# Two-block network on one core: attention pairs pipelined between dense units, output projections in a new order of units

## What is computed

```python
def first_block(x, c, ...):
    for i in range(DEPTH):
        mod = silu(c) @ ada_w[i] + ada_b[i]
        shift, scale, gate = jnp.split(mod, 3)
        h = rms_norm_f32(x, norm_g[i]) * (1.0 + scale) + shift
        out = retention_mixer(h, ...) if i == 0 else chunked_attention_mixer(h, ...)
        x = x + gate * out
...
def chunked_attention_mixer(h, w_in, q_g, k_g, rel_table, w_out):   # 16 heads of 128
    q, k, v, g = jnp.split(h @ w_in, 4, axis=-1)
    q, k = rms_norm_f32(q, q_g), rms_norm_f32(k, k_g)               # per head
    s = q @ k.T * scale + bias            # a chunk of 64 sees itself and 8 chunks before
    o = softmax(s) @ v * silu(g)
    return o @ w_out                      # 2048 -> 1024
...
        hm = rms_norm(x, norm_mlp[l]) @ mlp_w1[l]                   # 1024 -> 4096
        x = x + jnp.square(jax.nn.relu(hm)) @ mlp_w2[l]             # 4096 -> 1024
```

## Time and profile before

| | us |
|---|---|
| Time of the kernel, median of 3 | 2114.42 (2105.43 to 2114.66) |
| Profiled execution, its own time | 2116.99 |
| Its span from the first to the last instruction | 2114.9 |
| PE busy | 1928.5 (91%) |
| POOL busy | 1093.8 (52%) |
| DVE busy | 787.0 (37%) |
| ACT busy | 464.1 (22%) |
| Mean granted clock of TensorE | 0.941 |

### The profile page before, as it was taken

The page is one execution under the profiler, slowest core; times in us unless marked ns, Lnnn a source line. Parts: engine busy times, 40 slices in busy tenths (PEclk is TensorE's granted clock), DMA queues, the critical chain, the costliest instruction groups (busy, mean ns, idle before and its releaser), DMA issues.

```text
span 2114.9 us, 27134 instructions
## 1 busy us (share of the span) xinstructions
PE 1928.5 (91%) x9694; PEld 1580.0 (75%) x9694; DVE 787.0 (37%) x1413; ACT 464.1 (22%) x933; POOL 1093.8 (52%) x856
## 2 busy tenths in 40 slices
PE   4699999989899999999989899989899879999998
PEld 3588887868777877778768676877777658787776
DVE  4615323155423122322231384796433463102300
ACT  2211112100212122212220115644303322101200
POOL 2345454458443435343426557874063467667752
PEclk8799999999899999999999998999997989999999
DMA  8322222247222222221312331210021123233321
GB/s 285 127 70 75 69 84 65 79 139 253 70 81 68 60 69 80 67 63 55 89 49 79 85 89 50 61 29 23 1 90 50 40 80 99 82 97 90 99 81 48
DMA packets 276375, 172.92 MB, mean 82 GB/s; under 512 B 5792, under 2 KB 269856, under 8 KB 274272
## 3 DMA queue, kind: packets, MB, share of 16 engines
q1 hardware_dynamic: 269136, 148.92, 24.2%
q10 hardware_dynamic: 7184, 23.27, 3.1%
HBM read 169.93 MB, written 2.10 MB: 81 GB/s over the span
## 4 chain that ended last, share of the span: by engine, by line
PE 80%; DVE 12%; ACT 3%; issue 2%; DMA 1%; POOL 1%; DVEq 0%; ACTq 0%; POOLq 0%
PE acc L368 18%; PE acc L369 17%; PE acc L370 17%; PE st L401 3%; PE acc L390 3%; PE acc L391 3%; PE acc L392 3%; PE ob L1302 2%; PE ob L1234 2%; DVE conv_out L1974 2%; PE bc L434 2%; PE sc L1296 1%; DVE hn L482 1%; DMA x_tok<-in_x 1%; DVE att_scores L1916 1%
## 5 line engine op out<-in xcount | busy, mean ns | idle before, releaser
L664 POOL TENSOR_SCALAR wh<-raw 128x1024 fp32r<-128x1024 f32 x232 | 255.6, 1102 | 856.9 <-PE acc L370 535.5
L667 POOL TENSOR_TENSOR wl<-raw,wh 128x512 fp32r<-128x512 f32 x464 | 643.5, 1407 | 19.4
L368 PE MATMUL acc<-hh,wh 128*128 128x512 f32 x1120 | 458.3, 409 | 44.0 <-DVE ang L1813 13.9
L369 PE MATMUL acc<-hl,wh 128*128 128x512 f32 x1120 | 446.7, 399 | 0.0
L370 PE MATMUL acc<-hh,wl 128*128 128x512 f32 x1120 | 446.3, 398 | 0.0
L368 PEld LDWEIGHTS acc<-hh,wh 128*128 128x128 f32 x1120 | 216.6, 193 | 97.1 <-issue 45.3
L370 PEld LDWEIGHTS acc<-hh,wl 128*128 128x128 f32 x1120 | 216.7, 193 | 47.2
L369 PEld LDWEIGHTS acc<-hl,wh 128*128 128x128 f32 x1120 | 216.9, 194 | 43.8 <-issue 1.7
L368 PE MATMUL acc<-Yh,wh 128*128 128x512 f32 x512 | 205.2, 401 | 18.2 <-DVE mod L1794 8.2
L369 PE MATMUL acc<-Yl,wh 128*128 128x512 f32 x512 | 204.6, 400 | 0.0
L370 PE MATMUL acc<-Yh,wl 128*128 128x512 f32 x512 | 204.2, 399 | 0.0
(11 more groups left out here) (386 smaller groups left out, 2684.2 us busy)
## 6 DMA issues: line engine op xcount, KB each, us to landing
raw<-in_att_w_in SPq DMA_DIRECT2D x64, 512.0 KB, 4.0
raw<-in_mlp_w SPq DMA_DIRECT2D x64, 512.0 KB, 4.0
raw<-in_ret_w_in SPq DMA_DIRECT2D x48, 512.0 KB, 3.9
ada_w<-in_ada_w ACTq DMA_DIRECT2D x8, 1536.0 KB, 8.2
raw<-in_w_in SPq DMA_DIRECT2D x23, 512.0 KB, 3.8
ada_w<-in_ada_w SPq DMA_DIRECT2D x8, 1024.0 KB, 16.4
raw<-in_ret_w_out SPq DMA_DIRECT2D x16, 512.0 KB, 3.7
raw<-in_att_w_out SPq DMA_DIRECT2D x16, 512.0 KB, 3.6
```

Of the source, the lines that this page charges most:

```text
L368: e.matmul(bank[:, :], wh[:, s, k, :], rhs_high(k), start=(start and k == 0), stop=False)
L369: e.matmul(bank[:, :], wh[:, s, k, :], rhs_low(k), start=False, stop=False)
L664: e.tensor_scalar(wh[:, s, :, :], raw[:, s, :, :], 1.0, 1.0, ALU.mult, ALU.mult).then_inc(high_done, 1)
L667: low = e.tensor_tensor(wl[:, s, k0:k0 + KT // 2, :], raw[:, s, k0:k0 + KT // 2, :], wh[:, s, k0:k0 + KT // 2, :].bitcast(F32), ALU.subtract)
```

## The change

**Attention.** TensorE's scores, transposes and value products no longer stand in rows of their own but in gaps between the units. In a turn: unit 0, last two scores of the pair before and seven transposes of its first head; unit 1, sums, three transposes; unit 2, sums, value product of the first head, seven transposes of the second; unit 3, sums, three transposes; first quarter of `tok`, sums; second quarter, value product of the second head, spread; two quarters, spread, two scores; unit 6, two scores; unit 7, two scores of the second head. The transposes go through `ob`, the value products into `sc`. VectorE's and ScalarE's programs are cut into the same pieces and put in the matching order. The bias of the second head is loaded a turn later than before, behind that head's exponentials.

**Output projections.** In each turn the order of units is now bank 0 lower inputs, bank 1 lower inputs, bank 0 upper inputs, bank 1 upper inputs, and the loads follow. The first turn stands ahead of the loop; its lower halves wait only for the first eight tiles of `Y`, its upper halves for the last. In `att_out` the last pair's work stands behind the first and second unit, and the upper half of bank 0 waits for the last two tiles ahead of its seventh.

```diff
-        def product(e, bank, u, c, rhs_high, rhs_low, start=True, stop=True, k1=KT, inputs=None):
+        def product(e, bank, u, c, rhs_high, rhs_low, start=True, stop=True, k1=KT, inputs=None, late=None):
...
+                if late is not None and late[0] == k:
+                    e.wait_ge(*late[1])
...
-        def out_tensor(e, tag, ready):
+        def out_tensor(e, tag, free, ready, gaps=None, late=None):
             c = U[tag]
-            e.wait_ge(*ready)
-            with e.Fori(0, KT // 2) as i:
-                PE.enter(tag, i)
-                for b in range(2):
-                    e.wait_ge(*V.at(f"{tag}x{b}", i - 1))
-                    for half in range(2):
-                        product(e, acc[b], c + i * 4 + 2 * b + half, c + 2 * b + half,
+
+            def turn(i):
+                for half in range(2):
+                    for b in range(2):
+                        if half == 0:
+                            e.wait_ge(*(free[b] if isinstance(i, int) else V.at(f"{tag}x{b}", i - 1)))
+                        if b == 0 and isinstance(i, int):
+                            e.wait_ge(*ready[half])
+                        product(e, acc[b], c + i * 4 + 2 * half + b, c + 2 * half + b,
                                 lambda k: Yh[:, 8 * half + k, :], lambda k: Yl[:, 8 * half + k, :],
...
+                        if gaps is not None and half == 0 and isinstance(i, int):
+                            gaps[b]()
+
+            turn(0)
+            with e.Fori(1, KT // 2) as i:
+                turn(i)
...
-                    e.wait_ge(unit_used, c + i * 4 + 2 * b + 2)
+                    e.wait_ge(unit_used, c + i * 4 + b + 3)
...
-                        k0 = r0 + 8 * (j % 2)
-                        load(c + i * 4, c, i, rows(w, k0, k0 + 8, (i * 2 + j // 2) * P))
+                        k0 = r0 + 8 * (j // 2)
+                        load(c + i * 4, c, i, rows(w, k0, k0 + 8, (i * 2 + j % 2) * P))
...
             with e.Fori(1, AH // 2) as i:
                 AC.enter("att_scalar", i, 1)
-                att_qk(i, "a", None)
-                att_pv(i - 1, i, "a", None)
-                att_vg(i, "a")
+                att_evict(i, "a", 0)
+                att_turned(i, "a", 0, (0, 1))
+                att_exp(i, "a", 1)
+                load_bias(1, i * 2 + 1)
+                att_evict(i, "a", 1)
+                att_turned(i, "a", 0, (2, 3))
+                att_evict(i, "a", 2)
+                att_turned(i, "a", 1, (0, 1))
+                att_high(i - 1, i, "a", 0)
+                att_evict(i, "a", 3)
+                att_turned(i, "a", 1, (2, 3))
+                att_value(i, "a", 0)
+                att_high(i - 1, i, "a", 1)
+                att_value(i, "a", 1)
+                att_gate(i, "a", 0)
+                att_exp(i, "a", 0)
+                load_bias(0, i * 2 + 2)
+                att_gate(i, "a", 1)
                 AC.leave(AH // 2 - 1)
...
-            out_tensor(e, "ret_out", V.after("r_yl3", RH))
+            out_tensor(e, "ret_out", [V.after("r_g2", RH), V.after("r_g3", RH)],
+                       [V.after("r_yl3", RH // 2), V.after("r_yl3", RH)])
...
+                    if t == "a":
+                        if j == 0:
+                            att_scores(i, t, 1, 2)
+                            att_scores(i, t, 1, 3)
+                            att_turned(i, t, 0, 0)
+                            att_turned(i, t, 0, 1)
+                        if j == 1:
+                            att_turned(i, t, 0, 2)
+                            att_turned(i, t, 0, 3)
+                        if j == 2:
+                            att_values(i, t, 0)
+                            att_turned(i, t, 1, 0)
+                            att_turned(i, t, 1, 1)
+                        if j == 3:
+                            att_turned(i, t, 1, 2)
+                            att_turned(i, t, 1, 3)
...
+                tok(e, c + 4, U["att"] + 4, f"{t}v", [AC.at(f"{t}qk2", i), AC.at(f"{t}qk3", i)],
+                    between={0: last_sums, 1: values_and_spread})
+                e.wait_ge(*V.at(f"{t}k0", i))
+                spread(e, f"{t}bc1", c0=12)
+                att_scores(i, t, 0, 0)
+                att_scores(i, t, 0, 1)
+                e.wait_ge(*AC.at(f"{t}v0", i))
+                feat(e, acc[0], c + 6, U["att"] + 6)
+                att_scores(i, t, 0, 2)
+                att_scores(i, t, 0, 3)
+                e.wait_ge(*AC.at(f"{t}v1", i))
+                feat(e, acc[1], c + 7, U["att"] + 7)
+                att_scores(i, t, 1, 0)
+                att_scores(i, t, 1, 1)
...
-            out_tensor(e, "att_out", V.at("zyl1"))
...
+            out_tensor(e, "att_out", [V.at(f"ag{b}", AH // 2 - 1) for b in range(2)],
+                       [V.at("ayl1", AH // 4), V.at("ayl1", AH // 4 + 2)], [last_scores, last_values],
+                       (6, V.at("zyl1")))
...
-                out_tensor(e, f"mlp_out{half}", V.after(f"f{half}yl3", 4))
+                out_tensor(e, f"mlp_out{half}", [AC.after(f"f{half}r{b + 2}", 4) for b in range(2)],
+                           [V.after(f"f{half}yl3", 2), V.after(f"f{half}yl3", 4)])
...
+            def att_second(i, t):
+                att_key(i, t, 1)
+                e.wait_ge(bias_in[0], i * 32 + 32)
+                for n in range(NT):
+                    att_scores(i, t, 0, n)
+                att_maxima(t, 0)
+                att_gate(i, t, 0)
+                att_normalize(i, t, 0)
+                att_gate(i, t, 1)
+                e.wait_ge(bias_in[1], i * 32 + 32)
+                for n in range(2):
+                    att_scores(i, t, 1, n)
...
             with e.Fori(1, AH // 2) as i:
                 V.enter("att_vector", i, 1)
-                att_pv(i - 1, i, "a")
-                att_vg(i, "a", i)
+                att_first(i, "a")
+                att_out_value(i, "a", 0)
+                att_low(i - 1, i, "a", 0)
+                att_roots(i, "a")
+                att_out_value(i, "a", 1)
+                att_key(i, "a", 0)
+                att_low(i - 1, i, "a", 1)
+                att_second(i, "a")
                 V.leave(AH // 2 - 1)
```

More of the change, by code:

```diff
@@ L376, in feat, with tok @@
             product(e, bank, u, c, lambda k: hh[:, k, :], lambda k: hl[:, k, :], inputs=inputs)
-        def tok(e, u, c, tag, free, lh=hh, ll=hl, tiles=NT):
+        def tok(e, u, c, tag, free, lh=hh, ll=hl, tiles=NT, between=None):
             s = c % RING
@@ L396, in tok @@
                     last.then_inc(*PE.done(tag))
+                if between is not None and t in between:
+                    between[t]()
         def columns(e, x, c0, start, stop, name=None, n=NT, parts=P, of=None):
@@ L830, in load_bias, with att_evict @@
                      .then_inc(bias_in[h], 16)
[L832 removed]
+            def att_evict(i, t, j):
                 c = U["att"] + i * 8
[L834 to L841 removed]
@@ L861, in att_pv @@
[L861 to L871 removed]
+                dst = (aq, ak)[j // 2][:, j % 2, :]
@@ L1288, in att_pv, with last_sums @@
[L1288 to L1304 removed]
+                def last_sums():
+                    e.wait_ge(*AC.at(f"{t}sq3", i))
+                    columns(e, sq[:, 1, :], 12, True, True, f"{t}cols3")
@@ L1942, in _, with att_key, att_gate @@
-            att_vg(0, "p", 0)
+            def att_key(i, t, h):
+                e.wait_ge(*PE.at(f"{t}bc{h}", i))
+                step(e, e.tensor_tensor(ak[:, h, :], ak[:, h, :], bc[:, :], ALU.mult), V, f"{t}k{h}")
+            def att_gate(i, t, h):
+                e.wait_ge(*AC.at(f"{t}th{h}", i))
+                e.scalar_tensor_tensor(out=ag[:, h, :], in0=ag[:, h, :], scalar=1.0, in1=acc[h][:, :],
+                                       op0=ALU.add, op1=ALU.mult).then_inc(*V.done(f"{t}g{h}"))
@@ L1947, in _ @@
                 V.leave(AH // 2 - 1)
-            att_pv(AH // 2 - 1, 0, "z")
+            att_first(0, "z")
+            for h in range(2):
+                att_out_value(0, "z", h)
+                att_low(AH // 2 - 1, 0, "z", h)
             out_vector(e, "att_out", lambda n: mod[:, 1, 2, bass.ds(n, 1)])
```

248 lines of the change are left out of this document (132 added, 116 removed).

## The result

The changed kernel takes 2048.2 us (median of four executions, 2045.65 to 2050.88) against 2110.6 for the kernel before beside it: a ratio of 0.9713, with an interval of 0.9683 to 0.9742. The prediction was 2052.4 with a range of 2038 to 2070. The profiled execution of the changed kernel took 2050.88, 66.1 less than the 2116.99 of the profiled one of before.

What follows compares the result with a forecast made beforehand. TensorE, busy 91% of the span, was taken as the bound. Terms -44.8, -4.2, -6.3, -11.0 and +4.3 sum to -62.0: from the profiled 2116.99 us to 2055, or 2052.4 on the median's scale, range 2038 to 2070.

Steps and rivals of the forecast that it cites:

- Pair loop, -44.8 forecast: Attention's pair loop: each of seven turns drops from 68.36 to 62.0 us, -44.8 us in all.
- What was added for switches and short groups, 0.7: Cost added to each pair turn: 0.4 us for switches after sums, 0.3 for short groups starting alone.
- its own bounds of -38 to -50: Pair loop: -38 us with 1 us of waits a turn, -50 with no added cost at all.
- the last part of the theory above: Theory for the experiments: the loop's extra 10 us are a clock that fell in the old order, not the new.
- First pair, -4.2: Ahead of the pair loop: six of the first pair's eight score matmuls now lie between units, -4.2 us.
- Behind the last turn, -6.3: From the loop's end to attention's output projection: 18.3 us shrink to 11.2, half a clock fall counted, -6.3 (-8 to -4).
- Feed-forward, -11.0: Two feed-forward projections: the wait for the last low part and the slow start behind it go, 5.5 us each, -11.0.
- Retention, +4.3: Retention projection: early start given back by three residual waits; column sums run cold after 6 us idle; +4.3 us (0 to +6).
- The slack of 2 us: Pair loop: ScalarE finishes the last head's exponentials 2 us before unit 1 ends and wants it, the smallest slack found.
- rival 1: Pair loop: ScalarE's slack is spent, each turn waits 3 us more, 21 us in all, time 2073; chance 0.13.
- Rival 3: Pair loop: short groups make the clock fall with dense units behind; 2157 us at three slow units a turn; chance 0.04.

Runs made afterwards that it cites:

- run 5: The changed kernel with each pair turn's last two groups of sums, twenty transposes and both value products in one row behind unit 3: 2069.27 us, ratio 0.9835.
- run 6: The kernel before, unchanged, executed once more for its trace: 2102.46 us.
- run 2: The changed kernel with the retention and feed-forward projections put back to the old order, so only the attention part is new: 2050.59 us, ratio 0.9721.
- run 9: Relative to run 5, the first head's value product stands between the two heads' transposes: 2077.97 us, ratio 0.9839.
- Run 1: The kernel before with only the three output projections in the new order, attention pairs as they were: 2098.59 us, ratio 0.9957.
- runs 7 and 8: The changed kernel with fourteen, then thirty-two, small ScalarE activations a pair turn between head 1's exponentials and unit 1's eviction: 2046.93 us and 2048.44 us.
- run 3: The changed kernel, but in the retention projection only turn 0 keeps the new order; turns 1 to 3 take each bank whole: 2025.65 us, ratio 0.9613.
- run 4: The changed kernel with VectorE's second modulation sum of each retention projection turn moved behind residual 1: 2042.01 us, ratio 0.9674.

## Why the prediction was right, point by point

- **Pair loop, -44.8 forecast, -55.0 in the profiled executions.** The mechanism held: 60.50 us a turn, clock 1.00, no wait. The term was mis-sized by 1.5 us a turn. Transposes were priced at 2.4 to 2.7 us for twenty and take 1.94 (two groups of seven at 0.69, two of three at 0.28, by starts): the 0.96 us for seven was the length of merged records, which includes the way through the array. Eight scores were priced at 4.3, from products whose price held (2.24 and 2.16 us here), and take 3.54 by starts. What was added for switches and short groups, 0.7, is about 0.6; most of it lies in the units behind scores (5.68, 5.68 and 5.89 us instead of 5.45). The term also stands outside its own bounds of -38 to -50. So the last part of the theory above does not hold: the 68.36 us of the old turn, fall included, went into the forecast, and the extra 10 us are prices that were too high in the new one.
- **What the turn was made of before.** Of 68.36 - 60.50 = 7.86 us, 2.5 are the clock (68.36 against 65.88 in turns of the same kernel without a fall), 2.2 the row of small work (run 5 without a fall, 62.70, against 60.50) and 3.2 are left for the scores in one stretch. No run moved the scores alone, but their own rows agree: 7.29 us before against 3.54 and about 0.5 in the units behind them. The prediction spread the clock's part over values and transposes. It treated a fall in every turn as a property of the kernel, which run 6 shows it is not: against that execution the loop gained 464.2 - 423.5 = 40.7 us, less than the forecast. The median of before (2110.61) lies between the two traces, and so the gain of 62.4 by the medians came out at the forecast's 62.0 although the traces differ by 66.1. The time itself lies 4.2 us under the forecast of 2052.4. That closeness is in part luck: it rests on which executions fell into the sample, and on a loop term that was 10 us too small against 3.4 us that the retention term missed and 2.8 in a stage that had no term.
- **First pair, -4.2: -4.6.** The cause and the size were right.
- **Behind the last turn, -6.3: -5.4.** It was right in kind: three waits for ScalarE's copies (0.62, 1.17, 0.46), and the clock at 0.56 in the second value product, which cost 1.7 us. But the same program behind the same waits kept its clock in six of the eight traces of the new pairs. This row is from run 2, where the stretch takes 104.2 us and not 105.9:

```profile
1049.99 2.39 PE L1339 MATMUL sc<-att_probs_t,att_v 128*128 128x512 f32 x8 [0.46 <-ACT att_probs_t L871]
```

Taking half of the price of a fall was thus a fair way to price it. By the Trainium skill, TensorE: Matmul & The Clock Gate, section Part 4: PE-mode transpose, a transpose does not count as busy for the clock, and the prediction worked out from it a fall for sure and a term of -5.6; the trace of the changed kernel and that of run 9 agree, the six others do not.
- **Feed-forward, -11.0: -11.6,** with 397.8 to 398.2 us in the three traces of the old order and 386.6 to 386.7 in the eight of the new one.
- **Retention, +4.3: +7.7.** The mechanism was right: the three waits, forecast at 1.65 each, were 2.00, 1.76 and 1.73; the idle before the sums was 6.11 (forecast 6); the sums took 10.4 (forecast 10.5). What the term left out is that the clock fell behind two of the waits, which cost 3.1 us. Run 1, without these falls, has its modulation written at 544.81, against 541.44 and 540.45 in the two traces of before: +3.4 and +4.4.
- **The slack of 2 us** was that of ScalarE, which stood idle for 1.57 us there, and not that of TensorE: the eviction can come 5.6 us later still by runs 7 and 8. This only makes rival 1 less likely than the 0.13 that it was given. Rival 1 did not show.
- **Rival 3** (the clock falls because of short groups between dense units) did not show: in six traces with the new pairs the clock is 1.00 in all 42 turns, and they take 60.50 us, or 61.0 to 61.2 with the thirty-two activations. The opposite held: in three kernels with short groups gathered in a row (before, runs 5 and 9) the clock fell in some turns or all, and with the same groups spread between units of 5.5 us in none. What the Trainium skill says in TensorE: Matmul & The Clock Gate, section A second HAM failure mode: psum-queue depth-cycling, of small idles between groups had nothing to act on here, since TensorE does not wait in the changed loop and its clock is 1.00 throughout.
- **Left open:** the mixing and cross-attention stage, whose code is the same, takes 511.6 to 519.6 us in eleven traces. In the scores of its sparse attention (`st<-dsa_k,dsa_q`) the same groups start 6.0, 6.5 and 5.9 us apart in the changed kernel and 4.5, 3.4 and 3.2 in run 3. There the granted clock is 0.50 from 1373.30 to 1383.30 in the changed kernel and 1.00 from 1352.50 to 1362.50 in run 3, so the clock goes with most of the 7.3 us between these two. What makes it fall there was not tested.

## What to carry to other kernels

Price a stretch of small matmuls (sums, transposes, products of a few microseconds) by its own time plus a fall of the clock that may come in some turns and not in others; spread between dense units, as here between units of 5.5 us, they cost little more than their own time and the clock stayed up in every turn. When an accumulation is reordered so that both banks finish late, look at what the engine that frees the banks does between the first and the second: here two sums of 4 us turned a gain of 11 us into a loss of 8 (the stage ends at 530.03, 541.44 and 549.14 us in run 3, before and after), and keeping the new order for the first turn alone brought this stage 19 us forward. And before splitting a difference into terms, profile the kernel before twice: one trace of it held 14 us that another did not.

## What the runs showed of the hardware

- The granted clock falls in the middle of a stretch of transposes in which TensorE waits no longer than 0.4 us at a time, and whether it does changes from turn to turn of one loop: neighbouring turns with identical work took 65.88 and 66.98 us. The second value product behind the loop ran at 1.00 in six traces and at about half speed in two, behind the same transposes and the same waits.
- A wait of 1.73 to 2.00 us in a dense run sometimes costs a fall and sometimes not: the same three waits were followed by 0.50, 0.53 and 1.00 in the changed kernel and by 1.00 three times in run 1. A fall behind such a wait cost about 1.6 us, nearly as much as the wait. In the six traces with these waits (the changed kernel, runs 1, 5, 7, 8 and 9) a fall followed 4 of the 18.
- Twenty transposes of 128 columns with a 128-row fp32 operand take 1.94 us at full clock in groups of three and seven, 0.10 each; 48 records of one-column sums take 6.2 to 6.6 us when they start warm (granted clock 0.82 in run 3) and 10.4 at 0.50.
- A VectorE sum over 3072 fp32 columns takes 3.96 us right behind another such sum and 4.41 to 4.45 behind other work, as the first of each pair does and as all do in run 4's separated order.
